# First norm of a two-layer encoder: gain and offset applied after the turn, on partitions, and brought into the residual by GpSimd later

## What is computed

```
h = layer_norm(x, ln_in_g, ln_in_b)          # (x - mu) * rsqrt(var + eps) * g + b, over the 1024 features
for i in range(2):
    z = h @ w_in[i]                          # q | k | v | rnn input | rnn gate | two merge gates
    ...attention, two-way RG-LRU, merge...
    h = layer_norm(alpha * h + merged @ w_out[i], ln1_g[i], ln1_b[i])
    ...gated MLP with a width-3 conv, per-layer embedding...
    h = layer_norm(alpha * h + ffn + ple, ln2_g[i], ln2_b[i])
```

## Time and profile before

| what | value |
|---|---|
| median of 3 runs (lowest, highest) | 950.86 us (950.09, 951.03) |
| profiled execution, first to last instruction (its span) | 948.2 us |
| TensorE busy | 928.1 us, 98% of the span |
| VectorE busy | 724.2 us, 76% |
| ScalarE busy | 576.6 us, 61% |
| GpSimd busy | 1.4 us |

### The profile page before, as it was taken

One profiled execution on the slowest core, in us unless ns is written; L12 is line 12 of the kernel. 1 busy time (PEld: TensorE's weight loads), 2 busy tenths in 40 slices (PEclk: granted clock), 3 DMA queues, 4 the chain that ended last, 5 costly groups with the idle time before them and its releaser, 6 DMA issues.

```text
span 948.2 us, 12500 instructions
## 1 busy us (share of the span) xinstructions
PE 928.1 (98%) x5068; PEld 800.5 (84%) x5068; DVE 724.2 (76%) x971; ACT 576.6 (61%) x730; POOL 1.4 (0%) x9
## 2 busy tenths in 40 slices
PE   4999999999999999999999999999999999999996
PEld 3898888988888888888889889888888888888885
DVE  5887898787867867767867688888878676866755
ACT  4578889764356644555345889887435564545540
POOL 0000000000000000000000000000000000000000
PEclk9999999999999999999999999999999999999998
DMA  9546444584485655566453544456756656555621
GB/s 330 159 160 200 135 156 156 185 303 166 156 266 183 200 195 178 194 201 207 157 162 122 204 159 157 132 179 192 261 177 216 229 185 203 189 179 196 202 90 45
DMA packets 118457, 174.62 MB, mean 184 GB/s; under 512 B 3968, under 2 KB 78976, under 8 KB 117888
## 3 DMA queue, kind: packets, MB, share of 16 engines
q1 hardware_dynamic: 118256, 173.79, 55.1%
q10 hardware_dynamic: 144, 0.03, 0.0%
HBM read 172.76 MB, written 1.05 MB: 183 GB/s over the span
## 4 chain that ended last, share of the span: by engine, by line
PE 97%; DVE 1%; DMA 1%; ACT 0%; SPq 0%; issue 0%; DVEq 0%
PE ring L541 16%; PE ring L543 16%; PE ring L542 16%; PE ring L594 9%; PE ring L590 9%; PE ring L593 5%; PE ring L591 5%; PE misc L543 5%; PE misc L541 5%; PE misc L542 4%; PE misc L771 2%; PE misc L809 1%; PE misc L829 1%; PE ring L714 1%; DMA sb_hb<-in_w_in_dram 1%; PE ring L725 1%
## 5 line engine op out<-in xcount | busy, mean ns | idle before, releaser
L1245 DVE TENSOR_TENSOR sb_w_lo<-sb_raw,sb_w_hi 128x2048 fp32r<-128x2048 f32 x138 | 294.7, 2148 | 67.5 <-ACT sb_w_hi L925 67.4
L925 ACT CAST sb_w_hi<-sb_raw 128x2048 fp32r<-128x2048 f32 x138 | 246.2, 1795 | 16.1 <-DMA sb_raw<-in_w_proj_rnn_dram 3.9
L541 PE MATMUL ring<-sb_w_hi,sb_x_both 128*128 128x512 f32 x272 | 108.1, 397 | 0.0
L594 PE MATMUL ring<-sb_x_both,sb_w_hi 128*128 128x512 f32 x272 | 107.6, 396 | 0.0
L590 PE MATMUL ring<-sb_x_both,sb_w_hi 128*128 128x512 f32 x272 | 107.5, 395 | 0.0
L543 PE MATMUL ring<-sb_w_hi,sb_x_both 128*128 128x512 f32 x272 | 106.1, 390 | 0.0
L542 PE MATMUL ring<-sb_w_lo,sb_x_both 128*128 128x512 f32 x272 | 106.0, 390 | 0.0
L593 PE MATMUL ring<-sb_x_both,sb_w_lo 128*128 128x256 f32 x272 | 75.7, 278 | 0.0
L591 PE MATMUL ring<-sb_x_both,sb_w_lo 128*128 128x256 f32 x272 | 75.4, 277 | 0.0
L541 PE MATMUL ring<-sb_x_both,sb_w_hi 128*128 128x256 f32 x256 | 73.0, 285 | 0.0
L543 PE MATMUL ring<-sb_x_both,sb_w_lo 128*128 128x256 f32 x256 | 72.4, 283 | 0.0
(11 more groups left out here) (223 smaller groups left out, 2085.8 us busy)
## 6 DMA issues: line engine op xcount, KB each, us to landing
sb_raw<-in_w_in_dram SPq DMA_DIRECT2D x40, 1024.0 KB, 5.2
sb_raw<-in_w_up_dram SPq DMA_DIRECT2D x34, 1024.0 KB, 5.2
sb_raw<-in_w_down_dram SPq DMA_DIRECT2D x18, 1024.0 KB, 4.9
sb_raw<-in_w_proj_attn_dram SPq DMA_DIRECT2D x8, 1024.0 KB, 5.0
sb_raw<-in_w_proj_rnn_dram SPq DMA_DIRECT2D x8, 1024.0 KB, 5.1
sb_hb<-in_w_up_dram SPq DMA_DIRECT2D x8, 1024.0 KB, 5.2
sb_raw<-in_w_out_dram SPq DMA_DIRECT2D x6, 1024.0 KB, 6.0
sb_raw<-in_w_ple_gate_dram SPq DMA_DIRECT2D x6, 1024.0 KB, 5.7
```

What stands on the lines that cost most here:

```text
L541: nc.tensor.matmul(dst, lhs[0], rhs[0], start=first, stop=False)
L594: last = nc.tensor.matmul(bank_of(*key), hi[:, cols], x_both[:, k + 1], start=False, stop=k + 2 == KT)
L925: nc.scalar.copy(hi_at[home][:, at], raw_at[home][:, at]).then_inc(s_hi_part, 1)
L1245: nc.vector.tensor_tensor(lo_at[home][:, 0:size], raw_at[home][:, 0:size], hi_at[home][:, 0:size].bitcast(F32), ALU.subtract).then_inc(s_s ...
```

## The change

1. The first norm's gain and offset no longer come as 1 MB of copied rows ahead of the weights. One small load brings them as 16 rows of 128; TensorE turns them once, ScalarE copies them to `first_cols` [128, 16]: gain and offset of each feature, with the feature on the partition.
2. `first_norm` on VectorE only makes (x - mean) * root, one pass a half (`tensor_scalar`). The root comes from ScalarE (`Sqrt`), then a reciprocal and one Newton round.
3. Gain and offset go in when x is split: ScalarE makes the high part in four instructions of 128 columns a bank, with scale and bias from `first_cols`; VectorE makes the scaled value again in four instructions to a scratch tile and then the difference.
4. TensorE's list is arranged anew: both halves of a tile are turned together, and q1 part 0 of tile 0 goes behind q0 part 0 of tile 1. Its first high pass waits block by block.
5. The 1 MB load of gain and offset goes behind the fourth weight item. GpSimd then does h * gain, h + offset on both tiles (four instructions of 128x1024), and VectorE waits for it before the first `gate_input`.

In the diff below, the first `first_x_parts` and `first_root` are ScalarE's, `first_norm` and the second `first_x_parts` VectorE's; `norm_rest` and `x_parts` stay for all later norms.

```diff
-            load_first_norm(0, s_lnp_left)
-            load_first_norm(1, s_lnp)
+            sp.dma_start(first_rows, a["ln"][0:1].rearrange("a i (k p) -> (a i k) p", p=P)).then_inc(s_first_rows, 16)
...
                 for n in range(head + 3, ITEM[l, "gr0", 0]):
                     load_item(n)
+                    if (l, n) == (0, head + 3):
+                        load_norm(l, 0)
...
+            pool.wait_ge(s_lnp, 16)
+            pool.wait_ge(s_x_turned, value("x_turned", 0, 2 * TT))
+            for t in range(TT):
+                nc.gpsimd.tensor_tensor(h[:, t, :], h[:, t, :], lnp[:, 0, :], ALU.mult).then_inc(s_h_scaled, 1)
+            for t in range(TT):
+                pool.wait_ge(s_h_scaled, TT)
+                nc.gpsimd.tensor_tensor(h[:, t, :], h[:, t, :], lnp[:, 1, :], ALU.add).then_inc(s_h_scaled, 1)
...
+            def first_root(t):
+                act.wait_ge(s_first_step, FIRST_STEPS * t + 4)
+                nc.scalar.activation(mv[:, t, 2:3], mv[:, t, 2:3], ACT.Sqrt).then_inc(s_first_root, 1)
+
+            def first_x_parts(count, banks):
+                for i, (t, c) in enumerate(banks):
+                    act.wait_ge(s_x_turned, value("x_turned", 0, count + i + 1))
+                    for k in range(4):
+                        kk = 4 * c + k
+                        nc.scalar.activation(x_hi[:, kk, t * P:(t + 1) * P], misc[:, 2 * t + c, k * P:(k + 1) * P],
+                                             ACT.Identity, bias=first_cols[:, KT + kk:KT + kk + 1],
+                                             scale=first_cols[:, kk:kk + 1]).then_inc(s_first_hi if k < 3 else s_x_hi, 1)
...
+            def first_norm(t):
...
+                nc.vector.tensor_scalar(root, var, LN_EPS, None, ALU.add).then_inc(s_first_step, 1)
+                nc.vector.tensor_scalar(nhalf, var, LN_EPS, -0.5, ALU.add, ALU.mult).then_inc(s_first_step, 1)
+                dve.wait_ge(s_first_root, t + 1)
+                nc.vector.reciprocal(y, root).then_inc(s_first_step, 1)
...
+                for c in range(2):
                     at = h[:, t, 512 * c:512 * c + 512]
+                    nc.vector.tensor_scalar(at, at, mean, y, ALU.subtract, ALU.mult).then_inc(s_ln_norm, 1)
+
+            def first_x_parts(count, banks):
...
+                    for k in range(4):
+                        kk = 4 * c + k
+                        nc.vector.tensor_scalar(first_x[:, k * P:(k + 1) * P], misc[:, 2 * t + c, k * P:(k + 1) * P],
+                                                first_cols[:, kk:kk + 1], first_cols[:, KT + kk:KT + kk + 1],
+                                                ALU.mult, ALU.add).then_inc(s_first_scaled, 1)
...
+                    nc.vector.tensor_tensor(
+                        x_lo[:, 4 * c:4 * c + 4, t * P:(t + 1) * P], first_x.rearrange("p (k t) -> p k t", k=4),
+                        x_hi[:, 4 * c:4 * c + 4, t * P:(t + 1) * P].bitcast(F32), ALU.subtract).then_inc(s_x_ready, 1)
```

More of the change, by code:

```diff
@@ L230 @@
 LAST_STEPS = 14
+FIRST_STEPS = 8
 LN_REST = 12
@@ L329, in hybrid_encoder @@
         sm = sb("sm", [P, 6, GROUP])
+        first_rows = soft[0:2 * KT, 0, 0:P]
+        first_cols = sb("first_cols", [P, 2 * KT])
+        first_x = pT[:, :, :, :].rearrange("p a g t -> p (a g t)")[:, 0:512]
         ring = ctx.enter_context(nc.psum_tensor("ring", [P, 4, 512], F32))
@@ L768, in query_units, with turn @@
                     token_part(l, "q1", 1, t, x).then_inc(s_products, 1)
-            def turn(dst, src):
-                return nc.tensor.transpose(dst, src, ident[:])
+            def turn(dst, src, rows=P):
+                return nc.tensor.transpose(dst, src, ident[0:rows, 0:rows])
             def turn_rows(src, t, c):
@@ L1113, in _ @@
                 if l == 0:
+                    act.wait_ge(s_rows_turned, 1)
+                    nc.scalar.copy(first_cols[:], misc[:, 3, 0:2 * KT]).then_inc(s_first_cols, 1)
+                    first_root(0)
                     split_first_half()
-                x_parts(l, 0, [(0, 0)], 1.0)
-                if l == 0:
                     split_to(l, "q0", 0, 0)
-                x_parts(l, 1, [(0, 1)], 1.0)
-                if l == 0:
-                    split_to(l, "q1", 0, 0)
-                x_parts(l, 2, [(1, 0)], 1.0)
-                x_parts(l, 3, [(1, 1)], 1.0)
+                    act.wait_ge(s_first_cols, 1)
+                    first_x_parts(0, [(0, 0), (0, 1)])
+                    split_to(l, "q0", 1, 0)
+                    first_root(1)
+                    first_x_parts(2, [(1, 0), (1, 1)])
+                    split_to(l, "q1", 0, 0)
+                else:
+                    x_parts(l, 0, [(0, 0)], 1.0)
+                    x_parts(l, 1, [(0, 1)], 1.0)
+                    x_parts(l, 2, [(1, 0)], 1.0)
+                    x_parts(l, 3, [(1, 1)], 1.0)
                 if l == 0:
@@ L1308, in add_ffn, with step @@
-                norm_stats(l, 0, t, c)
+                if (t, c) == (0, 0):
+                    dve.wait_ge(s_ple_step, value("ple_step", l, 0))
+                dve.wait_ge(s_products, PRODUCT[l - 1, f"d{LAST}", (t, c)])
+                at = h[:, t, 512 * c:512 * c + 512]
+                nc.vector.tensor_tensor(at, at, misc[:, 2 * t + c, :], ALU.add).then_inc(s_added, 1)
+                dve.wait_ge(s_added, value("added", l - 1, 2 * t + c + 1))
+                norm_stats(l, 0, t, c)
+            def first_norm(t):
+                def step(k):
+                    dve.wait_ge(s_first_step, FIRST_STEPS * t + k)
+                dve.wait_ge(s_h[t], 16)
+                for c in range(2):
+                    nc.vector.bn_stats(st[:, t, c, :], h[:, t, 512 * c:512 * c + 512]).then_inc(s_first_step, 1)
+                step(2)
+                nc.vector.bn_aggr(mv[:, t, 0:2], st[:, t, 0:2]).then_inc(s_first_step, 1)
+                step(3)
+                mean, var = mv[:, t, 0:1], mv[:, t, 1:2]
+                root, nhalf, y, u = (mv[:, t, i:i + 1] for i in range(2, 6))
+                nc.vector.tensor_scalar(root, var, LN_EPS, None, ALU.add).then_inc(s_first_step, 1)
+                nc.vector.tensor_scalar(nhalf, var, LN_EPS, -0.5, ALU.add, ALU.mult).then_inc(s_first_step, 1)
+                dve.wait_ge(s_first_root, t + 1)
+                nc.vector.reciprocal(y, root).then_inc(s_first_step, 1)
+                step(6)
+                nc.vector.scalar_tensor_tensor(out=u, in0=y, scalar=y, in1=nhalf, op0=ALU.mult,
+                                               op1=ALU.mult).then_inc(s_first_step, 1)
+                step(7)
+                nc.vector.scalar_tensor_tensor(out=y, in0=u, scalar=1.5, in1=y, op0=ALU.add,
+                                               op1=ALU.mult).then_inc(s_first_step, 1)
+                step(8)
+                for c in range(2):
+                    at = h[:, t, 512 * c:512 * c + 512]
+                    nc.vector.tensor_scalar(at, at, mean, y, ALU.subtract, ALU.mult).then_inc(s_ln_norm, 1)
```

76 lines of the change are left out of this document (41 added, 35 removed).

## The result

| | before | after |
|---|---|---|
| median (lowest, highest), runs | 950.83 us (950.09, 951.03), 4 | 955.74 us (954.33, 956.28), 4 |
| profiled span | 948.2 us | 952.5 us |

The ratio is 1.0053, with a 95% interval of 1.0039 to 1.0068: slower by 0.5%. The prediction was 952.2, with 954.2 as its upper end, and it gave a loss of more than 0.2% a chance of 0.34: it had the direction, not the size. The profiled execution is the fastest of those runs, and its span has grown by 4.3 us.

What follows compares the result with a forecast made beforehand. TensorE, busy 98% of the span, was taken as the bound. Terms from tile 0's norm to item 2's cast reached 23.45 against 22.12, 1.3 us later: 950.86 + 1.3 = 952.2 us, range 950.2 to 954.2.

Steps and rivals of the forecast that it cites:

- The bound and the one moment: TensorE, busy 98% of the span, bounds the kernel; only when it passes 24 of 64 high-weight matmuls counts, before at 22.12.
- Tile 0: First norm and split: left half done at 8.0 instead of 9.33, ScalarE starting its split at 9.27.
- Four of 256 columns took 1.14; at half the columns from PSUM I take the same: VectorE's four scaling pieces of a bank cost 1.14; with the difference and two waits a bank is 1.9, before 0.69.
- Here is the step that decides. Item 2's cast: On ScalarE behind tile 1's eight pieces, the cast ends at 23.4; TensorE gets item 2 at 23.45, 1.3 us later.
- What I cost at nothing: Counted as free: the moved 1 MB load, GpSimd's four instructions (5 to 9 us), the table load before the exponential (1.28).
- My rival's price, 956: GpSimd beside VectorE, chance 0.08: if VectorE's weight differences lose all of GpSimd's 9 us, TensorE waits 4 us.
- The clock rival: TensorE's granted clock falls to 1.2 GHz after a wait of 1.7, adding 1.8 over eight matmuls: 954.0; chance 0.12.
- The sum: Terms from tile 0's norm to the hand-over of item 2 reach 23.45, less 22.12 before: 1.3 us later.
- two rivals that I held apart: Granted clock falling in TensorE's wait (chance 0.12, 954.0) and GpSimd slowing VectorE (chance 0.08, 956), both slower.
- the weights behind the `lnp` load: Removing 1 MB ahead of the weights, 2.8 us at 378 GB/s, lets the first half item be cast near 6.8, not 9.54.
- the exponential of `params`: It now waits for a table load of 1.28 on ScalarE, hidden by 1.5 of cover before TensorE wants item 5.
- The drain: Rival at the root's table load: another 1.38 us of drain, 1.4 more, 953.6; chance 0.04.

Runs made afterwards that it cites:

- e1: Changed kernel without GpSimd's four instructions, so the residual misses gain and offset; 953.48 us, ratio 1.0027.
- e2: Changed kernel with item 2's cast ahead of tile 1 on ScalarE and q1 part 0 ahead of q0 part 0 on TensorE again; 954.75 us, ratio 1.004.
- e3: Changed kernel with eight useless 512-column matmuls between tile 1's high and low pass, filling TensorE's wait; 954.49 us, ratio 1.0043.
- e9: Changed kernel without GpSimd's four instructions and with eight idle matmuls in TensorE's wait for tile 1's first low part; 952.4 us, ratio 1.0021.
- e6: Kernel before the change with only the split of x in 128-column pieces, scale 1 and offset 0; 954.63 us, ratio 1.0042.
- e7: Changed kernel with item 2's cast ahead of tile 1 and the residual's gain and offset on VectorE instead of GpSimd; 951.11 us, ratio 1.0006.
- e10: As e8, but the residual's gain and offset on GpSimd again; 954.62 us, ratio 1.0045.
- e4: Changed kernel with the root by the old guess and three Newton rounds on VectorE instead of ScalarE's Sqrt; 954.56 us, ratio 1.0043.
- e8: As e7, with tile 1's statistics ahead of tile 0's low parts and its root ahead of item 2's cast; 949.75 us, ratio 0.9996.

## Why the prediction was wrong

**The bound and the one moment: right.** All of the loss lies before 43 us, and over 40 to 938 us TensorE is still busy throughout.

**Tile 0: nearly right.** The left half was normed by 7.8 (forecast 8.0), but ScalarE began the pieces at 9.61 instead of 9.27, since its cast of the second half of item 0 waited for its DMA and began only at 8.66. I had both casts done before x was turned. ScalarE's bank took 1.51 (1.56). VectorE's took 2.2 from bank to bank, not 1.9: the term "Four of 256 columns took 1.14; at half the columns from PSUM I take the same" measured 1.36, and each hand-over 0.1. Statistics of tile 1 began at 15.43, outside my 14.3 to 15.2, and ScalarE's pieces of tile 1 at 19.42 instead of 18.5.

**"Here is the step that decides. Item 2's cast": the wrong wait.** The cast ended at 24.1 (forecast 23.4), and TensorE came to item 2 only at 25.87, when item 0 was done. I had let TensorE do "item 0 for tile 1 between" without a sum of its own. That pass needs VectorE's low part of bank (1, 0), and VectorE takes the bank up only when ScalarE is through with it. By my own terms the low part came at 18.5 + 1.56 + 1.9 = 22.0, 1.4 ahead of the cast; TensorE had it at 24.03. Of these 2.0 us, 0.9 is the later start, 0.77 GpSimd, the rest hand-overs and VectorE's pieces. So without GpSimd it would have come at 23.3, and by e1's rows it came at 23.61, with TensorE waiting for it and not for the cast. e2 shows that the cast was not what held TensorE: with it out of the way the wait was still 2.29.

**"What I cost at nothing": GpSimd's four instructions, the first step that failed.** I had them at 5 to 9 us; they took 12.4 (20.98 to 33.33). I looked for their effect on the five weight differences, with 5 us of cover. They doubled two of those (2.28 to 4.49), and in the changed kernel that was covered, as said. But they started at 20.98, when their load had landed, and so met the one difference that TensorE waited for: 0.69 became 1.46 in one execution and 2.52 in another. The Trainium skill (SBUF — State Buffer, Who interferes with whom) has the rule that the prediction cited, and the trace agrees with it; the size that it leaves open was 2.3 us of median here (955.74 against e1's 953.48). I did not apply it to the difference of x, to which the change had given its second SBUF input. My rival's price, 956, lies close to the measured time by luck: it was worked out for weight differences that make TensorE wait, and in the changed kernel none did.

**The clock rival, given 0.12: it came in, the second step that failed.** I had 1.8 for its price, and 1.75 was measured. I had set its point at "a wait hardly longer than that of 1.59" and forecast one of 1.7; with GpSimd it was 2.55, but e1, without GpSimd, has one of 1.77, and the clock fell there too. With the wait filled by matmuls it stayed at 1.00 in the profiles of e3 and e9. What else it takes besides a wait stays open: e6's 2.79 brought no fall.

**The sum.** Forecast +1.3, rows +4.3. The 3.0 between are 1.75 of clock, 0.77 of GpSimd on the low part, and 0.5 net of the rest: 0.9 for the late start of tile 1 and 0.4 for hand-overs and VectorE's dearer banks, less 0.6 by which my own terms had the low part and its four matmuls ahead of the cast, and less 0.2 because I subtracted the timeline's 22.12, at which the turn of tile 1 was still running, and not the chain's 22.36. The median lost 4.9 where the span lost 4.3; the first profile is the fastest run and caught the milder collision. So I had the right moment, a later 25th matmul, and the wrong wait ahead of it, and two rivals that I held apart came in together. GpSimd lengthened the wait after which the clock fell, but e1 shows that the fall did not need it.

**Right:** TensorE busy throughout from 40 to 938 us in both; the weights behind the `lnp` load; the exponential of `params`, at 43.17 behind its table load, without a gap in TensorE. The drain had no part: at the first root the table load started at 5.08 and the `Sqrt` at 6.37, 1.29 later, as in the earlier trace rows.

## What to carry to other kernels

Work moved to an idle GpSimd isn't free if it reads and writes SBUF while VectorE has instructions with two SBUF inputs: in the first profile VectorE lost 5.8 us (2 x 2.2 on weight differences, 0.77 and 0.59 on parts of x), more than the four instructions would have cost it (2.35 for two in e7, 4.7 for four). Here it was better to put them on VectorE, where it waits anyway. Ask too whether the change gives a VectorE instruction its second SBUF input. When a sum says which of several waits ends last, write out every operand of the waiting matmuls, the low part too; and give a wait of two microseconds or so in front of a dense stretch a fair chance of the clock's price as well as its own (1.75 us here). A cheaper norm that turns one instruction of 512 columns a bank into four of 128, on ScalarE and on VectorE, has to earn back its own price first (e6: 4.2 us in the span); in the best of the orders tried it only broke even.

## What the runs showed that I had not expected

- VectorE's slowdown beside GpSimd depends on the form: 128x512 with two SBUF inputs 0.69 to between 1.28 and 2.52, 128x2048 2.28 to 4.49, but 128x128 from PSUM with per-partition operands four in 1.36 in both cases. The traces look like turns, instruction by instruction, though GpSimd's times in a profile are rough: in the changed kernel the first weight difference ended 2.15 us after the GpSimd instruction it had met (28.93, 31.08), the next 2.14 after the next one (33.34, 35.48), where one alone takes 2.28. GpSimd seems to have waited in turn: of its two additions, which have one shape, one took 2.73 and the other, which began under a weight difference, 4.44. Smaller GpSimd instructions might then hold VectorE up for less; no run tried it.
- In the six profiles that have one, the clock's fall lasted 3.4 us (23.88 to 27.30 in the change, 25.00 to 28.42 in e1, 26.21 to 29.62 in e10) and began between 0.15 before and 1.4 after TensorE had resumed. Waits of 1.77, 2.23, 2.29, 2.55, 2.59 and 3.61 us were followed by it; waits of 0.67, 0.68, 1.19, 1.59 and, in e6, of 2.79 were not, nor was another of 2.59 in e4, ahead of the turn of tile 1. The length of the wait alone does not decide.
- The first rise of the clock came anywhere from 11.26 (e4) to 19.38 us (e10), for one and the same kernel at 17.06 and 19.23 (the change, twice). These are the times of the first clock records in the traces. The column PEclk shows 1.00 ahead of them as well, but the matmuls don't: in e8, with the rise at 11.99, four of 512 columns took 2.02 us at 10.12 and 1.18 at 13.37. A late rise moved tile 1 by up to 1.5 us (e10 against e8), which should add to the scatter of the medians here.
